# A two-layer decoder step on one core: gate projections moved from a stage of their own into the attention's slots, in halves of 24 matmuls

## The reference

```python
# even layer
q, k, v, f_logit, u_g, v_g = split(h @ w_in_even)           # widths 512,512,512,8,512,512
logf = log_sigmoid(f_logit + b_forget); F = cumsum(logf_all)
a = softmax(q.k/8 + F_q - F_k, causal) @ v_all              # prompt: own keys; sample: pages + own
out_b = u_g * (tril(w_s) @ layer_norm(v_g) + b_s)           # per chunk of 128, 8 groups
x = x + concat(a, out_b) @ w_out_even
# odd layer
q, k, v, gate_b, gate_c, h_in = split(h @ w_in_odd)         # six times 512
z = q.k/8; a = exp(log_sigmoid(z) + sum over later keys of log_sigmoid(-z)) @ v_all   # stick-breaking
u = gate_c * h_in; conv = three taps over u (with state); out_d = gate_b * conv
x = x + concat(a, out_d) @ w_out_odd
# after each: x = x + relu(h @ w_up)^2 @ w_down              # 1024 -> 4096 -> 1024
```

## Time and profile before

| | us |
|---|---|
| median of 3 runs | 1768.82 (1766.14 to 1770.13) |
| the profiled execution's own time | 1765.29 |
| its span, first to last instruction | 1763.6 |
| TensorE busy | 1564.6 (89%) |
| VectorE, ScalarE, GpSimd busy | 762.9, 515.4, 53.9 |
| even layer: units, sums and turns, from 54.7 | to 203.3 |
| even layer: slots and cuts | 203.3 to 375.3 |
| odd layer: projections after the first pair | 883.3 to 1027.2 |
| odd layer: slots and cuts | 1032.0 to 1248.9 |

### The profile page before, as it was taken

The page is one execution under the profiler, slowest core; times in us unless marked ns, Lnnn a source line. Parts: engine busy times, 40 slices in busy tenths (PEclk is TensorE's granted clock), DMA queues, the critical chain, the costliest instruction groups (busy, mean ns, idle before and its releaser), DMA issues.

```text
span 1763.6 us, 31756 instructions
## 1 busy us (share of the span) xinstructions
PE 1564.6 (89%) x12022; PEld 1450.0 (82%) x12022; DVE 762.9 (43%) x1175; ACT 515.4 (29%) x828; POOL 53.9 (3%) x124
## 2 busy tenths in 40 slices
PE   4999888878899999999899977666889999999994
PEld 3999755568899999999799964443789999999994
DVE  5344444534544343433523545555254433434334
ACT  3222133322333131322322134454133322313120
POOL 4310000000000000000000000000000000000000
PEclk9999899979899999999899997877889999999997
DMA  4323367722122232232125254564122222222221
GB/s 117 99 79 87 114 198 230 231 71 82 50 83 84 78 89 84 77 90 75 58 84 155 73 162 136 171 182 120 48 72 60 84 83 84 84 84 83 84 72 54
DMA packets 239070, 178.59 MB, mean 101 GB/s; under 512 B 9860, under 2 KB 203464, under 8 KB 238986
## 3 DMA queue, kind: packets, MB, share of 16 engines
q1 hardware_dynamic: 234282, 168.62, 32.9%
q0 software_dynamic: 4704, 8.88, 1.6%
HBM read 170.20 MB, written 7.26 MB: 101 GB/s over the span
## 4 chain that ended last, share of the span: by engine, by line
PE 82%; DVE 7%; ACT 3%; SPq 3%; issue 2%; DMA 1%; DVEq 0%; POOL 0%; POOLq 0%; ACTq 0%
PE BP L1252 64%; PE BP L1267 5%; PE BK L1405 2%; PE BD L1512 2%; PE BD L1484 1%; PE BP L1456 1%; PE BP L1443 1%; DVE PP L1058 1%; PE BK L1465 1%; DVE WL L750 1%; SPq L361 1%; SPq L345 1%; SPq L362 1%; ACT WH L488 1%; SPq L349 1%
## 5 line engine op out<-in xcount | busy, mean ns | idle before, releaser
L1252 PE MATMUL BP<-HH,WH 128*128 128x288 f32 x1792 | 386.9, 298 | 18.7 <-DVE ffL L788 7.9
L1252 PE MATMUL BP<-HH,WL 128*128 128x288 f32 x1792 | 385.8, 297 | 0.0
L1252 PE MATMUL BP<-HL,WH 128*128 128x288 f32 x1792 | 385.6, 297 | 0.0
L1252 PEld LDWEIGHTS BP<-HH,WH 128*128 128x128 f32 x1792 | 291.2, 191 | 20.2 <-ACT TMP L527 8.3
L1252 PEld LDWEIGHTS BP<-HH,WL 128*128 128x128 f32 x1792 | 291.4, 191 | 0.0
L1252 PEld LDWEIGHTS BP<-HL,WH 128*128 128x128 f32 x1792 | 290.9, 190 | 0.0
L750 DVE TENSOR_TENSOR WL<-WR,WH 128x1024 fp32r<-128x1024 f32 x188 | 230.0, 1225 | 95.2 <-ACT WH L488 53.4
L498 ACT ACTIVATE WH<-WR 128x1024 fp32r<-128x1024 f32 x173 | 181.9, 1052 | 243.3 <-PE BP L1252 240.4
L1252 PE MATMUL BP<-ffH,WH 128*128 128x288 f32 x1024 | 218.9, 295 | 0.0
L1252 PE MATMUL BP<-ffL,WH 128*128 128x288 f32 x1024 | 218.3, 294 | 0.0
L1252 PE MATMUL BP<-ffH,WL 128*128 128x288 f32 x1024 | 216.9, 293 | 0.0
(11 more groups left out here) (286 smaller groups left out, 1379.2 us busy)
## 6 DMA issues: line engine op xcount, KB each, us to landing
WR<-in_w_up_dram SPq DMA_DIRECT2D x64, 512.0 KB, 4.1
WR<-in_w_down_dram SPq DMA_DIRECT2D x64, 512.0 KB, 3.8
KR<-in_cache_fox_k_dram SPq DMA_DIRECT2D x64, 256.0 KB, 3.0
KR<-in_cache_sb_k_dram SPq DMA_DIRECT2D x64, 256.0 KB, 2.9
WR<-in_w_in_odd_dram SPq DMA_DIRECT2D x24, 512.0 KB, 3.8
WR<-in_w_in_even_dram SPq DMA_DIRECT2D x20, 512.0 KB, 3.9
VR<-in_cache_fox_v_dram SPq DMA_DIRECT2D x32, 256.0 KB, 3.0
VW<-in_cache_fox_v_dram SPq DMA_DIRECT2D x32, 256.0 KB, 3.0
```

The costliest lines, as they stand in the source:

```text
L1252: last = M(B[2 * u + h][:, 0:TH], w[u][:, k, :], x[:, k, h * TH:(h + 1) * TH], start=(k == 0 and n == 0), stop=(k == KT - 1 and n == 2))
```

## The change

- Gate units leave their stage. The even layer keeps four of its eight ahead (the rows `v_g` for the layer norm), its other four (`u_g`) and all twelve of the odd layer (`gate_c`, `h_in`, `gate_b` for each of four row tiles in turn) become *side units*, each in two halves of 24 matmuls (288 columns each) in the slots: one half per slot in even slots 0 to 7; two per slot in odd slots 0 to 5, one in odd slots 6 to 17 (`halves_of`, `half_unit`). In the odd layer queries, keys and values come first, straight after the norm.
- The halves have a bank of their own, BU. Page turns have one bank, BK, instead of two; weighted values use BK too.
- The halves need WH and WL, so VW is gone: value pages go into VR, eight pages, two groups in turn; `load_v` waits until the group two before has been used, and stands later in SyncE's loop.
- Side weights are loaded and cut within the slots (`load_side`, `next_weights`); the first output unit's cut is made there too, one cut is left behind the last slot.
- The order in the slots changes on all engines: on TensorE `scores(k-2)` now stands first and `turn_weights(k-3)` behind the first half; `sample_values(p,0)` moves to the end of slot o = 1; in the even layer `sample_top` and `sample_exp` move from o = 0 to o = 1. In the odd layer ScalarE makes three of four page copies and both copies of the turned weights.
- Gating and convolution run on VectorE in the slots, on halves straight out of BU (`gate_half`, `conv_in`, `conv`); the splits into HH and HL of gates and attention come late (`SIDE_OUT`, `ATT_OUT`).
- GpSimd's gathers and the wait of TensorE for them are as before.

```diff
-        n_b = [2 * CT, 3 * CT]
-        G_QKV = [G_IN[L] + n_b[L] for L in range(2)]
+        n_first, n_side = [CT, 0], [CT, 3 * CT]
+        G_QKV = [G_IN[L] + n_first[L] for L in range(2)]
+        G_SIDE = [G_QKV[L] + 3 * CT for L in range(2)]
...
+        def halves_of(L, k):
+            if L == 0:
+                return [(k // 2, k % 2)] if k < 2 * CT else []
+            if k < 6:
+                return [(k, 0), (k, 1)]
+            return [(6 + (k - 6) // 2, k % 2)] if k < 18 else []
...
                 def load_v(p, g):
-                    if L == 0 and p == 0 and g == 0:
-                        sp.wait_ge(S["sgu_out"], CT)
-                    if p == 0 and g == 2:
-                        sp.wait_ge(S["unit_done"], G_OUT[L] + 1)
-                    if L + p > 0:
-                        sp.wait_ge(S["v_used"], (NPAIR * L + p - 1) * 4 + g + 1)
+                    t = 4 * (NPAIR * L + p) + g
+                    if t == 0:
+                        sp.wait_ge(S["sgu_step"], CT)
+                    if t >= 2:
+                        sp.wait_ge(S["v_used"], t - 1)
...
                         for g in range(4):
-                            if s == (4 * p + 3 + g if p else 1 + g) and not (L == 1 and p == 0 and g < 2):
+                            if p == 0 and g < 2:
+                                if L == 0 and s == 1 + g:
+                                    load_v(p, g)
+                            elif s == 4 * p + 4 + g:
                                 load_v(p, g)
...
-                pe.wait_ge(S["sgu_low" if L == 0 else "conv_low"], CT)
+                if L == 0:
+                    pe.wait_ge(S["sgu_step"], CT)
+                else:
+                    pe.wait_ge(S["se_set"], 1)
...
                 def page(n):
-                    if n >= 2:
-                        pe.wait_ge(S["kt_dve" if n % 2 else "kt_act"], NB * PG // 2 * L + n // 2)
+                    if n >= 1:
+                        name, count = page_copied(L, n - 1)
+                        pe.wait_ge(S[name], count)
...
+                def half_unit(j, h):
+                    g = G_SIDE[L] + j
+                    u = g % 2
+                    if h == 0:
+                        pe.wait_ge(S["w_low"], g + 3)
+                    if L + j + h > 0:
+                        pe.wait_ge(S["half_out"], half_count(L, j, h))
+                    for k in range(KT):
+                        for n, (w, x) in enumerate(((WH, HH), (WH, HL), (WL, HH))):
+                            last = M(BU[:, 0:TH], w[u][:, k, :], x[:, k, h * TH:(h + 1) * TH],
+                                     start=(k == 0 and n == 0), stop=(k == KT - 1 and n == 2))
+                    last.then_inc(S["unit_done" if h else "half_done"], 1)
...
# TensorE's slot after the change
+                    if 2 <= k < NTASK + 2:
+                        scores(k - 2)
                     if p >= 0 and o == 3:
                         weighted_values(p)
+                    if 2 <= k < NGRP + 2 and k % 2 == 0:
+                        page_scores(k - 2)
+                    if k < NGRP:
+                        if p >= 0 and o == 3:
+                            pe.wait_ge(S["av_out"], CT * L + p + 1)
+                        page(4 * k)
+                    for j, h in halves[0:1]:
+                        half_unit(j, h)
+                    if k < NGRP:
+                        page(4 * k + 1)
                     if 3 <= k < NTASK + 3:
                         turn_weights(k - 3)
                     if 2 <= k < NGRP + 2 and k % 2 == 0:
                         page_scores(k - 1)
+                    if p >= 0 and o == 3:
+                        sample_values(p, 2)
                     if p >= 0 and o == 1:
                         turn_sample(p)
+                    if k < NGRP:
+                        page(4 * k + 2)
                     if p >= 0 and o == 2:
                         sample_values(p, 1)
                     if p >= 0 and o == 3:
                         sample_values(p, 3)
+                    for j, h in halves[1:2]:
+                        half_unit(j, h)
+                    if p >= 0 and o == 1:
+                        turn_new(p)
                     if k < NGRP:
                         page(4 * k + 3)
+                    if p >= 0 and o == 1:
+                        sample_values(p, 0)
```

More of the change, by code:

```diff
@@ new lines, in conv @@
+                def conv(c, j):
+                    dve.wait_ge(S["half_out"], half_count(L, j, 1) + 1)
+                    V.tensor_copy(tail[:, c, 0:2], UE[:, NP:NP + 2])
+                    last = V.tensor_copy(tail[:, c, 2:2 + 2 * NB].rearrange("p (b r) -> p b r", r=2), SE[:, c, :, NT:NT + 2])
+                    if c == CT - 1:
+                        last.then_inc(S["tail_set"], 1)
+                    t = RES[:, c, :]
+                    tp, ts = t[:, 0:NP], t[:, NP:T].rearrange("p (b t) -> p b t", t=NT)
+                    for i in range(NCV):
+                        w = vec[:, CONV_V + i * CT + c:CONV_V + i * CT + c + 1]
+                        up, us = UE[:, i:i + NP], SE[:, c, :, i:i + NT]
+                        if i == 0:
+                            V.tensor_scalar(tp, up, w, None, ALU.mult)
+                            V.tensor_scalar(ts, us, w, None, ALU.mult).then_inc(S["conv_step"], 1)
+                        else:
+                            V.scalar_tensor_tensor(tp, up, w, tp, ALU.mult, ALU.add)
+                            V.scalar_tensor_tensor(ts, us, w, ts, ALU.mult, ALU.add).then_inc(S["conv_step"], 1)
+                        dve.wait_ge(S["conv_step"], c * NCV + i + 1)
@@ new lines, in _ @@
+                    halves = halves_of(L, k)
+                    if L == 0:
+                        if 2 <= k < NTASK + 2:
+                            row_top(k - 2)
+                        if p >= 0 and o == 1:
+                            sample_top(p)
+                        if k < NGRP:
+                            copy_page(4 * k + 1)
+                        for j, h in halves:
+                            side_half(j, h)
+                        if 2 <= k < NTASK + 2:
+                            row_scale(k - 2)
+                        if 3 <= k < NTASK + 3:
+                            turned_out(k - 3)
+                        if p >= 0 and o == 1:
+                            sample_scale(p)
+                            spread_blocks(p)
+                        if k < NGRP:
+                            copy_page(4 * k + 3)
+                        next_weights(k)
+                        if k == 0:
@@ L1380, in _ @@
                 else:
-                    unit_loop(pe, unit(HH, HL), G_QKV[1], 2)
                     pe.wait_ge(S["state_in"], 16)
@@ L1531, in _ @@
+                    for j, h in halves[0:1]:
+                        half_unit(j, h)
+                    if k < NGRP:
+                        page(4 * k + 1)
                     if 3 <= k < NTASK + 3:
                         turn_weights(k - 3)
-                    if 2 <= k < NTASK + 2:
-                        scores(k - 2)
                     if 2 <= k < NGRP + 2 and k % 2 == 0:
-                        page_scores(k - 2)
                         page_scores(k - 1)
-                    if k < NGRP:
-                        page(4 * k)
-                        free_page(4 * k + 1, p if p >= 0 and o == 3 else None)
+                    if p >= 0 and o == 3:
+                        sample_values(p, 2)
@@ L1549, in _ @@
+                    if p >= 0 and o == 1:
+                        turn_new(p)
                     if k < NGRP:
-                        page(4 * k + 2)
                         page(4 * k + 3)
```

469 lines of the change are left out of this document (268 added, 201 removed).

## The result

The changed kernel takes 1760.2 us (median of 5 runs, 1759.6 to 1761.7) against 1768.8; the ratio is 0.9954 [0.9939, 0.9968]. It is faster, by 0.5%, where 3.8% was forecast: 1760 lies outside the range of 1670 to 1740. The span went from 1763.6 to 1758.2 us, the forecast was 1695.9. Of all executions reported here one was slow (e11, 2182 us at a granted clock of 0.64); it is left out of e11's figures.

What follows compares the result with a forecast made beforehand. TensorE was taken as the bound (82% of the chain), except in attention slots, held by SyncE's loads or the weight turns. Even +9.7, odd -83.9, allowance +6.5 gave -67.7 us: 1701 us by the median, range 1670 to 1740.

Steps and rivals of the forecast that it cites:

- 6 odd projections: Odd layer's projections: twelve units of 6.40 us leave, with no gather wait there, -76.8 us.
- allowance: Added to the whole sum for what such sums leave out, low clock in places: +6.5 us.
- Step 4: Even slots 8 to 15, no halves: page-load queue stays at 8.74 us; value-load hold-ups and a longer sample slot, +5.6 us.
- Step 3: Even slots 1 to 7 with seven halves: own work, halves and waits sum to +12.2 us, ends +5 and +22.4.
- Step 2: Hand-over to even attention and slot 0 with its half: an idle gap goes, -3.4 us, ends 0 and -6.
- Step 5: Even tail after slot 15: late value pages against one weight cut already made, +1.0 us, ends -1.2 and +5.
- Steps 7 and 8: Odd slot 0 with two halves, +3.4 us; odd slots 1 to 5 with ten halves, +15.7 us.
- Rival (c): Slower: value loads waiting for buffers hold back key pages and halves' weights in the shared queue; 1793 us at 3.3 a batch; chance 0.04.
- Step 9: Odd slots 6 to 15, one half each: weight turn no longer waits, TensorE's work decides, 10.75 us a slot, -15.8 us.
- Rival (a): Odd slots keep their chain, each half coming on top of 12.3 us: 47.5 us in slots 6 to 15, 1748; chance 0.17.
- Step 10: Odd tail, slot 16 and from slot 17 on: 33.5 us instead of 43.9, -10.4 us, ends -4 and -15.
- Step 1: Even projections: four units leave, -25.6 us, but TensorE waits 18.0 for gathers and restarts cold, +1.9; -5.7 us.

Runs made afterwards that it cites:

- e11: e4 with the cuts of the halves' weights on ScalarE and VectorE shrunk to one element each: 1722.2 us, ratio 0.9740 to the kernel before.
- e4: Changed kernel with 3 of the 24 matmuls of each half computed, outputs incomplete: 1724.8 us, ratio 0.9738 to the kernel before.
- e10: e9 with sample_values(p,0) in its old slot and no value loads after the first two groups: 1678.5 us, ratio 0.9503 to the kernel before.
- e6: Changed kernel with value pages loaded for the first two groups of a layer alone: 1747.7 us, ratio 0.9891 to the kernel before.
- e9: e5 with 3 of the 24 matmuls of each half computed, outputs incomplete: 1709.0 us, ratio 0.9665 to the kernel before.
- e3: Changed kernel with even-layer sample maxima and exponentials a slot earlier, and sample_values(p,0) moved to the middle of slot o=2: 1778.5 us, ratio 1.0068.
- e7: e3 with value pages loaded for the first two groups of a layer alone: 1727.9 us, ratio 0.9772 to the kernel before.
- e13: e10 with all value pages loaded again: 1746.0 us, ratio 0.9885 to the kernel before.
- e5: e2 with the samples' maxima and exponentials one slot earlier in the even layer, sample_values(p,0) unmoved: 1736.5 us, ratio 0.9809 to the kernel before.
- e2: Changed kernel with page turns, halves and weighted values taking banks BK and BU in turn: 1748.1 us, ratio 0.9894 to the kernel before.
- e1: Changed kernel with the lf_raw turn and its sums issued later, behind gate-tile turns and two query units: 1739.9 us, ratio 0.9848.
- e8: Changed kernel with lf_raw turned later, banks in turn, even-layer maxima early, and odd-layer new-key turns ahead of the value units: 1718.1 us, ratio 0.9708.
- e12: e8 with value loads from the third group on issued by GpSimd: 1707.9 us, ratio 0.9673 to the kernel before.

## Why the prediction was wrong

The direction and both projections were right; the size of the attention stages was not. By its own steps, against the stretches above:

| step | forecast | measured |
|---|---|---|
| 1 even projections | -5.7 | -6.1 |
| 2 hand-over, even slot 0 | -3.4 | +0.4 |
| 3 even slots 1 to 7 | +12.2 | +21.8 |
| 4 even slots 8 to 15 | +5.6 | +20.2 |
| 5 even tail | +1.0 | +5.1 |
| 6 odd projections | -76.8 | -77.0 |
| 7 odd slot 0 | +3.4 | +7.3 |
| 8 odd slots 1 to 5 | +15.7 | +20.6 |
| 9 odd slots 6 to 15 | -15.8 | +1.2 |
| 10 odd tail | -10.4 | +0.4 |
| allowance | +6.5 | (in the others) |

The steps from 2 to 5 miss by 32.1 us, 7 to 10 by 36.6; less the allowance these are the 62 us of the span.

**Step 4 failed.** It priced two events, 0.8 us of a held queue and a slot o=1 of 10.2 us, and called 8.74 us of page loads the floor. The slots take 11.25 us on average where the forecast makes 9.4, and SyncE is not the bound there any more: it stands for 22.4 us in these eight slots, waiting for buffers. What took its place is a chain through three engines, which the step did not follow to its end: maxima, exponentials, `turn_sample`, its copies, `turn_new`, PTN, `sample_values(p,0)`, all in one slot, with a page copy between neighbouring turns; and the idle time that it made lowered the clock. The ladder of runs takes the even stage down: 219.5, with two banks 213.3, maxima early 197.6, seven eighths of the halves out 190.5, the old place of `sample_values` without its loads 169.0; against 168.6 before. So 6.2 us are the bank, 15.7 the maxima, 7.1 the halves (e4 had 10.6), and 21.5 the eight pages and the placement that goes with them. The order of the steps matters in such a ladder, and its last value meets that of the kernel before in part by balance (see e10).

**Step 3 was mis-sized in its own work.** For slots 1 to 4 it put TensorE's own matmuls at 15.3 us at full clock; after the change they are 18.9 (33.16 busy, less 14.29 on the line of the halves) at clock 0.93. The earlier trace rows has 20.91 at 0.90. The idle time of slots 1 to 7 is 9.6 us, where 3.6 was put for slots 1 to 4 and 2.3 for slots 5 and 6.

**The smaller steps.** Step 2 misses by 3.8 us, and even slot 0 has three waits for page copies, 3.8 us in sum, where the step named one copy of 0.69 us. Step 5 misses by 4.1; the tail has 5.1 us of waits for value pages and 3.9 for the samples' exponentials. Steps 7 and 8 had no waits at all in their sums; TensorE idles for 3.5 and 5.3 us there, and they miss by 3.9 and 4.9.

**Rival (c) named the right resource and the wrong price.** It looked for late landings bare on TensorE. These are 11.1 us in sum, under the 15 us at which the forecast was to be wrong. Eight pages cost more than that once the other losses are out: loads with the early place cost 11 us on the changed kernel (e6), loads and early place together 29 on top of e9 (e10). With the old place the loads cost 50 (e3 against e7) and 67 (e13 against e10). The largest loss of the samples' chain, the late maxima, was not forced by the eight pages: e5 undoes it and keeps them.

**Step 9 failed in size, and in what it took to decide.** The chain of the prompt's weights did shrink: its wait fell from 37.9 us to 6.7, and the clock rose from 0.82 to 0.95, over the 0.9 that was to show it. By the rule of the Trainium skill (TensorE: Matmul & The Clock Gate, Part 1) activity lifts the clock; this trace agrees, and e4 from the other side: with an eighth of each half the odd stage is at 0.79 instead of 0.92. Rival (a), 15.5 us a slot, did not occur: 12.45. But the step took TensorE's work as 9.8 us a slot and it is 10.92; and 0.95 of waits, where there are 1.53. That makes 11.2 and 5.8 us of 17.0. Own work had been carried over from even slots at clock 0.98 less an estimate, 6.6 us; without the halves it is 7.5, and the earlier trace rows has 8.7 us in the odd slots themselves at 0.82. The step also said that TensorE's work decides, since the loop of one slot through the engines sums to 7.5 us. By that, with an eighth of each half the ten slots would take some 80 us (an estimate: 6.6, 0.4 and 0.95 a slot). e4 has 113.1, with TensorE idle for 25.0 of them, the largest wait being that for PP, 7.1 us. So waits between the engines hold these slots near 11 us, and halves that lie in them are partly free.

**Step 10** had the tail lose 10.4 us; it gained 0.4. Nothing that was to shorten it was tried by itself. Of TensorE's 17.7 idle us in it 6.0 are waits for value pages and 4.5 the one for the last cut; without value loads the tail takes 39.8 us instead of 44.3 (e6). Most of the rest are waits in the chains of the samples (RD 2.7, exponentials 1.9, PTN 0.8) and of the prompt (PP 1.7).

The odd stage goes down the same ladder, from its first page turn: 246.4, with two banks 238.8 (e2; 243.8 in e5, with the same code), seven eighths of the halves out 225.2, old place without value loads 217.0; against 213.9 before. So the halves are 18.6 us of it (23.3 by e4) and the eight pages with their placement 8.2; what is left, 3.1 us, and the share of the banks are within the scatter of 5.

Step 1 was right in mechanism and sum, and could have said more: e1 shows that the 17 us, which the forecast accepted as the price, were there for an edit of order.

## What to carry to other kernels

When buffers are cut, follow the release as well as the landing: what must be used earlier, so that the next load isn't late, goes to the end of some chain; here 11 us of waits stood for a placement without which 50 to 67 us were lost. When work moves into gaps, count all steps of one slot that now depend on one another across engines, hop by hop, and not only the busy time of each engine. And before a sum accepts a wait that an edit uncovers, look for independent work that stands behind it: 19 of some 43 us between the changed kernel and e8 were there.

## What the runs showed of the hardware

The same four turns of a page take 1.06 us at 307.87, at a granted clock of 0.50, and 0.60 at 310.24, at 1.00 (above): the two levels of TensorE's clock, 1.2 and 2.4 GHz, 2.4 us apart in one slot. Work laid into gaps returned part of its cost through the clock: 21 of 66 us in the odd layer.

GpSimd issued the value pages of e12 1.14 us apart (300.35, 301.49), near SyncE's 1.09; they landed 3.4 and 3.8 us after their issue (medians, even and odd), against 3.0 and 3.2 where SyncE issued all of them (the changed kernel). GpSimd's queue is thus as quick to issue, and its pages landed 0.4 to 0.6 us later:

```profile
300.35 0.54 POOL L555 DMA_DIRECT2D VR<-in_cache_fox_v_dram  x1 [0.60 <-issue]
301.49 0.54 POOL L555 DMA_DIRECT2D VR<-in_cache_fox_v_dram  x1 [0.59 <-issue]
```
